# Modulation sums moved wholly beside the first block, their first steps on ScalarE, and the first gated feed-forward's first row group by seven

## Chip, cores and metric

One NeuronCore of a Trainium2 chip runs one program (five engines, 16 DMA engines). The metric is the device time of one execution in microseconds (us).

## What is computed

Two blocks in float32 on x of 512 tokens by 1024 channels. The first block (gMLP and HGRN2 branches, mixed) ends in a feed-forward and a norm:

```
x = x + mix @ w_out
h = rmsnorm(x, norm_ffn)
x = x + square(relu(h @ w_ff1)) @ w_ff2          # 4096 hidden columns
return rmsnorm(x, final_norm)
```

The second has two layers, each a gated feed-forward, a mixer, and a gated feed-forward, all modulated by a vector c:

```
c_act = silu(c)
mod = c_act @ w_ada[l] + b_ada[l]                # 9 x 1024 numbers a layer: shift, scale, gate
h = rmsnorm(x, norm_g[l, 0]) * (1 + sc1) + sh1
x = x + 0.5 * g1 * ((silu(h @ wg) * (h @ wu)) @ wd)   # 2816 hidden columns
```

The modulation of both layers depends on c alone, so it can be computed beside other work.

## The kernel before

**Products.** Every product in float32 is three matmuls: high by high, low by high, high by low, where high is a rounding to fp32r (ScalarE: w_hi, b_hi) and low the rest (VectorE: w_lo, b_lo). The channels lie on the partitions, so a matmul has 512 tokens as its columns. The work is cut into units of 256 output columns by 1024 rows of weights: 1 MB of weights, 48 matmuls of 512 columns. For a unit SP loads w_raw (one of two slots), ScalarE makes w_hi in two halves (`weight_hi`, L1509), VectorE w_lo in two halves (`weight_lo`, L2307), TensorE multiplies into one of two pairs of PSUM banks (`product`, L741). Semaphores count: raw_landed, hi_done, lo_done, chunk_done, out_taken. SP loads unit u+2 when w_lo of unit u is done.

**The first block's feed-forward** is four groups of eight units (`hidden_group`: TensorE L1071, ScalarE L1892, VectorE L2853). In the first four of a group ScalarE takes the output up (Relu), makes w_hi half, squares it into hid and b_hi, makes the other half; VectorE makes w_lo half, b_lo (L2860), w_lo half. The other four units are down products; the first of them takes its rows k in order and waits for b_lo k // 2 before rows k. The last group's four down units are in `residual` (L2387), which adds into xT, and beside it adds up the squares of the next norm (`add_squares`, `add_sixth`). The last of them (`product_tail`, L794) is split so that the norm's sum of squares (L812, L814) runs inside it. The second block's norm "00" is folded with the first block's final norm; plain_ssq is the other sum that this takes, and `final_norm_step` (L2879, eight steps) scales xT afterwards.

**The modulation sums.** For each of 8 quarters q (2304 columns each) there are 8 steps: `ada_acc = ada_in * c_act[:, 0]` (L2770), then seven times `ada_acc += ada_in * c_act[:, k]` (L2773), all on VectorE. Then a turn (L2782, transpose in 32 x 32 blocks) and a reduction (L2789), a small matmul (L1063, `modulation`) and a bias (`add_bias`, L2798). POOL loads ada_in (1.15 MB, two buffers): load o waits for step o-2 (L710). When the steps are made is written out by hand: ADA[u] is the number of steps done by the end of place u, where places 0 to 3 are the output projection's units, 4 to 35 the 32 units of the first block's feed-forward, and from 36 on the first gated feed-forward. `ada_part(u)` (L2820) stands at the end of VectorE's work for a unit. ADA stands at 56 for places 31 to 35, and the last eight steps lie in the first gated feed-forward.

**Gated feed-forwards.** 2816 columns are three groups of 8, 8 and 6 chunks of 128: a group has n/2 pairs (a gate unit, an up unit) and then four down units. A pair can be computed plainly or "by seven" (Strassen's seven block products in Winograd's form, `seven_products` L1151): 14 block products of 12 matmuls with 256 columns instead of 96 with 512. This takes sums of weight blocks and of token blocks t1 to t4 and sums of the results on VectorE. `seven_from(l, j, g)` says from which pair of a group this is done: from the third pair in the first group (two plain pairs let the token sums be made), from the first in the others. The exception is the very first group (0, 0, 0): all four pairs are plain there, the eight last modulation steps and the final norm's steps lie beside them, and the token sums are made from a_hi + a_lo beside its down units (`product_sums`).

The order of instructions on each engine is the order of the program; all waits are explicit, so what stands behind a waiting instruction on its engine waits too.

## Time and profile before

| | us |
|---|---|
| runs, median (lowest to highest) | 2638.23 (2637.9 to 2640.33) |
| the profiled execution, its own time | 2636.77 |
| its span, first to last instruction | 2635.0 |
| TensorE busy | 2615.9 (99%), 15665 matmuls |
| VectorE (DVE) busy | 1836.9 (70%) |
| ScalarE (ACT) busy | 1141.4 (43%) |
| GpSimd (POOL) busy | 71.3 (3%) |

Shares of busy time are means over all stages. The granted TensorE clock is 1.000 of full in the mean. In the text PE is TensorE, PEld its weight loads, DVE VectorE, ACT ScalarE, POOL GpSimd, SP the engine that issues weight loads. "Idle before" in a row is the engine's idle time before the instructions, with what ended it. In a timeline a row is start, duration of the merged instructions, engine, line, operation, out<-in, shapes, count.

### The profile page before, as it was taken

To read this page: it belongs to the slowest core of one execution; us is meant where nothing else is said; L and a number is where in the kernel's file an instruction comes from. 1 tells how busy PE (TensorE), PEld (TensorE's weight loads), DVE (VectorE), ACT (ScalarE), POOL (GpSimd) and SP (SyncE) were. 2 spreads that over 40 slices of the span, in tenths; PEclk is the share of its full clock that TensorE was granted. 3 is DMA by queue.
4 is the path that set the end of the run, shared out by engine and by line. 5 is a ranking of instruction groups with operands and counts; after the bars stand their busy time and mean duration, and the time that the engine had idled before them with its cause. 6 is when DMAs were issued, how large, how long until landed. Compare 5 with 4: busy or idle time off the path is not lost.

```text
span 2635.0 us, 38697 instructions
## 1 busy us (share of the span) xinstructions
PE 2615.9 (99%) x15665; PEld 2302.0 (87%) x15665; DVE 1836.9 (70%) x2347; ACT 1141.4 (43%) x1594; POOL 71.3 (3%) x119
## 2 busy tenths in 40 slices
PE   8999999999999999999999999999999999999999
PEld 7888888888888889998878999989899988898998
DVE  7777653688988779586467685877677654676775
ACT  5566532433224425344455443445343422453432
POOL 1000000000000000000400000000000000000000
PEclk9999999999999999999999999999999999999999
DMA  4111223568887433323212333223233222233332
GB/s 146 65 64 64 83 94 96 185 241 303 306 305 280 162 135 110 96 89 110 64 53 92 112 96 113 89 90 111 95 114 97 96 96 96 87 106 104 105 96 80
DMA packets 257945, 324.56 MB, mean 123 GB/s; under 512 B 5766, under 2 KB 248708, under 8 KB 249604
## 3 DMA queue, kind: packets, MB, share of 16 engines
q1 hardware_dynamic: 245904, 245.12, 28.9%
q0 software_dynamic: 9216, 75.50, 7.6%
q8 instruction: 108, 1.77, 0.3%
q10 hardware_dynamic: 2676, 1.84, 0.2%
q14 instruction: 41, 0.34, 0.0%
HBM read 320.34 MB, written 2.10 MB: 122 GB/s over the span
## 4 chain that ended last, share of the span: by engine, by line
PE 96%; DVE 2%; ACT 1%; issue 0%; DMA 0%; DVEq 0%; ACTq 0%
PE po L764 16%; PE po L766 16%; PE po L765 16%; PE po L1140 7%; PE po L1142 7%; PE po L1141 7%; PE po L833 1%; PE pm L1140 1%; PE pm L1141 1%; PE pm L1142 1%; PE po L835 1%; PE po L848 1%; PE po L881 1%; PE po L867 1%; PE po L876 1%; PE po L934 1%
## 5 line engine op out<-in xcount | busy, mean ns | idle before, releaser
L2312 DVE TENSOR_TENSOR w_lo<-w_raw,w_hi 128x1024 fp32r<-128x1024 f32 x336 | 400.1, 1223 | 146.1 <-ACT w_hi L1517 139.4
L1517 ACT ACTIVATE w_hi<-w_raw 128x1024 fp32r<-128x1024 f32 x290 | 293.0, 1051 | 463.7 <-PE po L766 425.7
L764 PE MATMUL po<-b_hi,w_hi 128*128 128x512 f32 x1008 | 393.0, 390 | 0.0
L765 PE MATMUL po<-b_lo,w_hi 128*128 128x512 f32 x1008 | 392.3, 389 | 0.0
L766 PE MATMUL po<-b_hi,w_lo 128*128 128x512 f32 x1008 | 392.2, 389 | 0.0
L764 PE MATMUL po<-a_hi,w_hi 128*128 128x512 f32 x752 | 293.1, 390 | 0.0
L766 PE MATMUL po<-a_hi,w_lo 128*128 128x512 f32 x752 | 292.6, 389 | 0.0
L765 PE MATMUL po<-a_lo,w_hi 128*128 128x512 f32 x752 | 292.6, 389 | 0.0
L764 PEld LDWEIGHTS po<-b_hi,w_hi 128*128 128x128 f32 x1008 | 189.3, 188 | 39.6 <-DVE b_lo L2860 0.6
L766 PEld LDWEIGHTS po<-b_hi,w_lo 128*128 128x128 f32 x1008 | 189.2, 188 | 39.5
L765 PEld LDWEIGHTS po<-b_lo,w_hi 128*128 128x128 f32 x1008 | 189.3, 188 | 38.6
L2401 DVE SCALAR_TENSOR_TENSOR xT<-po,gate,xT 128x512 f32<-128x512 f32 x104 | 74.0, 734 | 182.1 <-PE po L766 173.1
L766 PEld LDWEIGHTS po<-a_hi,w_lo 128*128 128x128 f32 x752 | 141.2, 188 | 29.3
L765 PEld LDWEIGHTS po<-a_lo,w_hi 128*128 128x128 f32 x752 | 141.2, 188 | 29.2
L764 PEld LDWEIGHTS po<-a_hi,w_hi 128*128 128x128 f32 x752 | 141.2, 188 | 29.2
L1928 ACT ACTIVATE w_hi<-w_raw 128x1024 fp32r<-128x1024 f32 x102 | 106.7, 1056 | 131.9 <-PE po L766 74.0
L2773 DVE SCALAR_TENSOR_TENSOR ada_acc<-ada_in,c_act,ada_acc 128x2304 f32<-128x2304 f32 x56 | 146.4, 2614 | 23.2 <-DMA ada_in<-in_w_ada_dram 21.3
L2929 DVE TENSOR_TENSOR w_lo<-w_raw,w_hi 128x1024 fp32r<-128x1024 f32 x102 | 124.1, 1220 | 36.6 <-ACT w_hi L1928 36.6
L1970 ACT ACTIVATE ev<-po 128x256 f32<-128x256 f32 x204 | 76.8, 377 | 145.0 <-PE po L1142 144.0
L1928 ACT ACTIVATE x_hi<-w_raw 128x1024 fp32r<-128x1024 f32 x102 | 104.2, 1054 | 49.9 <-DVE w_raw L2953 48.8
L2929 DVE TENSOR_TENSOR x_lo<-w_raw,x_hi 128x1024 fp32r<-128x1024 f32 x102 | 122.3, 1218 | 4.7 <-ACT x_hi L1928 4.2
L1140 PE MATMUL po<-t_hi,w_hi 128*128 128x256 f32 x408 | 115.7, 284 | 0.0
(486 smaller groups left out, 6306.8 us busy)
## 6 DMA issues: line engine op xcount, KB each, us to landing
ada_in<-in_w_ada_dram POOLq DMA_DIRECT2D x64, 1152.0 KB, 5.6
w_raw<-in_ffn_wg_dram SPq DMA_DIRECT2D x44, 1024.0 KB, 5.3
w_raw<-in_ffn_wu_dram SPq DMA_DIRECT2D x44, 1024.0 KB, 5.3
w_raw<-in_w_ff_dram SPq DMA_DIRECT2D x32, 1024.0 KB, 5.3
w_raw<-in_ffn_wd_dram SPq DMA_DIRECT2D x32, 1024.0 KB, 5.2
w_raw<-in_w_in_dram SPq DMA_DIRECT2D x27, 1024.0 KB, 5.0
w_raw<-in_ffn_wd_dram SPq DMA_DIRECT2D x16, 768.0 KB, 4.5
w_raw<-in_w_in_c_dram SPq DMA_DIRECT2D x12, 1024.0 KB, 5.1
```

The lines of the kernel that those rows point to most:

```text
L764: pe.matmul(o, wh, hi[:, k, :], start=(k == ks[0]), stop=False)
L765: pe.matmul(o, wh, lo[:, k, :], start=False, stop=False)
L766: mm = pe.matmul(o, wl, hi[:, k, :], start=False, stop=(k == ks[-1]))
L1140: pe.matmul(o, wh[:, c], hi[:, k, :], start=(start and k == 0), stop=False, skip_group_check=True)
L1141: pe.matmul(o, wh[:, c], lo[:, k, :], start=False, stop=False, skip_group_check=True)
L1142: mm = pe.matmul(o, wl[:, c], hi[:, k, :], start=False, stop=(k == 3), skip_group_check=True)
L1517: act.activation(w_hi[:, s, part], w_raw[:, s, part], ACT.Copy).then_inc(hi_done, 1)
L1928: ins = act.activation(batch_out(ring_hi(batch), batch), batch_raw(batch), ACT.Copy)
L1970: act.activation(ev[:, 1, q * QT:(q + 1) * QT], first_bank(s), ACT.Copy)\
L2312: dve.tensor_tensor(w_lo[:, s, part], w_raw[:, s, part], w_hi[:, s, part].bitcast(F32), ALU.subtract).then_inc(lo_done, 1)
L2773: ins = dve.scalar_tensor_tensor(ada_acc[:, :], ada_in[:, k % 2, :], c_act[:, k:k + 1], ada_acc[:, :], ALU.mult, ALU.add)
L2929: ins = dve.tensor_tensor(batch_out(ring_lo(batch), batch), batch_raw(batch), batch_out(ring_hi(batch), batch).bitcast(F32), ALU.subtract)
```

## The change

1. The eight first steps of the modulation sums go from VectorE to ScalarE (`ada_start`): one before the norm "ffn", seven at the end of ScalarE's work for one unit each. POOL's load after next and VectorE's step 1 now wait for them.
2. ADA is new: 2, 4, 5, 5, 6, 9, then two more at each place from 6 (11) to 32 (63), 64 at 33. The last turn is at place 33, the last reduction at 34 (beside the last down units of the first block).
3. The group (0, 0, 0) goes like the other first groups: pairs 3 and 4 by seven, token sums from the norm's rows (`raw_sums`, `sums_hi`, `sums_lo`). `product_sums` and its ScalarE part go. The final norm's steps 0 to 3 stand behind `sums_lo`, 4 to 7 behind the last low block before the first pair by seven.
4. The ScalarE loop over three hidden groups is written out; plain_rstd has a place of its own.

```diff
     def seven_from(l, j, g):
-        if (l, j, g) == (0, 0, 0):
-            return GROUPS[g] // 2
         return PLAIN_PAIRS if g == 0 else 0
...
-    ADA = [1, 2, 3, 3, 4, 5, 7, 9, 10, 13, 15, 17, 18, 21, 23, 25, 26, 29, 31, 33, 34, 37, 39, 40, 41, 43, 45, 48, 49, 51, 53, 56, 56, 56, 56, 56, 57, 58, 60, 62, 64, 64, 64, 64]
+    ADA = [2, 4, 5, 5, 6, 9] + [11 + 2 * n for n in range(27)] + [64, 64, 64]
+    ADA_END = 33
...
                 elif o >= 2:
-                    pool.wait_ge(s_ada, o - 1)
+                    qp, kp = (o - 2) // DK, (o - 2) % DK
+                    if kp == 0:
+                        pool.wait_ge(s_ada_act, ada_first.after("a0", qp))
+                    else:
+                        pool.wait_ge(s_ada, ada.after(f"a{kp}", qp))
...
+            def ada_start(q):
+
+                act.wait_ge(ada_landed[0], q * 8 * DK + 16)
+                if q:
+                    act.wait_ge(s_asum, asum.after("tr", q - 1))
+                act.activation(ada_acc[:, :], ada_in[:, 0, :], ACT.Copy, scale=c_act[:, 0:1])\
+                    .then_inc(s_ada_act, ada_first.one("a0"))
+
+            ada_start(0)
             norm_halves("ffn", U_OUT)
 
+            ADA_START = {ada_unit(DK * q) + 1: q for q in range(1, 2 * FFG)}
...
+                    if ADA_FF + 8 * g + k in ADA_START:
+                        ada_start(ADA_START[ADA_FF + 8 * g + k])
...
             def add_ada(q, k):
 
                 dve.wait_ge(ada_landed[k % 2], at(q, 8 * DK, 16 * (k // 2 + 1)))
-                if k == 0:
...
+                if k == 1:
+                    dve.wait_ge(s_ada_act, ada_first.after("a0", q))
                 else:
                     dve.wait_ge(s_ada, ada.after(f"a{k - 1}", q))
...
-                    add_ada(q, k)
+                    if k:
+                        add_ada(q, k)
+                if u == ADA_END:
+                    turn_ada(2 * FFG - 1)
+                if u == ADA_END + 1:
+                    sum_ada(2 * FFG - 1)
...
                     if last:
                         block_lo(3, l, j, g, i + 1)
+                        if (l, j, g) == (0, 0, 0):
+                            for k in range(DK // 2, DK):
+                                final_norm_step(k)
                         continue
...
                     if i == 0:
                         sums_lo(l, j)
+                        if (l, j, g) == (0, 0, 0):
+                            for k in range(DK // 2):
+                                final_norm_step(k)
```

With this ADA the seven later first steps fall on places 6, 10, 14, 18, 22, 26 and 30: by turns the third hidden unit and the third down unit of each group. Steps 1 and 2 of the same quarter and the reduction of the quarter before fall on the same place on VectorE.

## Rows read from the trace of the kernel before

**Rows 1.** The page's chain that ended last, by engine.

```profile
PE 96%; DVE 2%; ACT 1%; issue 0%; DMA 0%; DVEq 0%; ACTq 0%
```

**Rows 2.** Windows: stretch; length, busy time and count by engine, clock, DMA share.

```profile
583.88:605.64 21.76, 21.76 (x99) 18.01 (x98) 18.38 (x13) 4.02 (x4) 2.64 (x5) 1.00 0.83 296
1429.80:1451.56 21.76, 21.76 (x97) 18.02 (x96) 18.52 (x25) 12.94 (x18) 0.00 (x0) 1.00 0.30 96
1451.56:1491.87 40.31, 40.31 (x337) 40.31 (x336) 30.72 (x42) 21.91 (x34) 0.00 (x0) 1.00 0.40 131
1004.11:1085.03 80.92, 80.92 (x675) 80.78 (x674) 65.90 (x93) 42.75 (x66) 0.00 (x0) 1.00 0.37 118
1535.42:1616.05 80.63, 80.63 (x673) 80.63 (x672) 65.09 (x92) 43.49 (x66) 0.00 (x0) 1.00 0.37 118
```

**Rows 3.** Groups by line on VectorE: count, busy us, mean ns.

```profile
L2773 DVE SCALAR_TENSOR_TENSOR ada_acc<-ada_in,c_act,ada_acc 128x2304 f32<-128x2304 f32 x56 | 146.4, 2614 | 23.2 <-DMA ada_in<-in_w_ada_dram 21.3
...
L2782 DVE STREAM_TRANSPOSE ada_tr<-ada_acc 128x2304 f32<-128x2304 f32 x8 | 20.6, 2575 | 0.1
L2789 DVE TENSOR_REDUCE ada_red<-ada_tr 128x72 f32<-128x2304 f32 x8 | 20.4, 2546 | 0.1
...
L2883 DVE SCALAR_TENSOR_TENSOR xT<-xT,cols,plain 128x512 f32<-128x512 f32 x8 | 5.5, 745 | 0.0
```

**Rows 4.** Timeline of ScalarE, third hidden unit of the last group.

```profile
814.42 1.03 ACT L1897 ACTIVATE ev<-po 128x1024 f32<-128x1024 f32 x1 [6.06 <-PE po L766]
...
817.24 1.05 ACT L1903 ACTIVATE b_hi<-ev 128x1024 fp32r<-128x1024 f32 x1
818.19 1.05 ACT L1517 ACTIVATE w_hi<-w_raw 128x1024 fp32r<-128x1024 f32 x1
```

**Rows 5.** Groups by line and shape on ScalarE.

```profile
L1517 ACT ACTIVATE w_hi<-w_raw 128x1024 fp32r<-128x1024 f32 x290 | 293.0, 1051 | 463.7 <-PE po L766 425.7 <-PE po L848 21.0 <-PE po L881 12.6
...
L1530 ACT ACTIVATE sq<-xT 128x512 f32<-128x512 f32 x49 | 28.5, 620 | 31.1 <-DVE xT L2400 16.9 <-DVE xT L2401 14.2
```

**Rows 6.** Timelines at 486 us; landings of L580 there, of L711 there and at 472; the page's median.

```profile
486.18 1.41 DVE L2770 TENSOR_SCALAR ada_acc<-ada_in,c_act 128x2304 f32<-128x2304 f32 x1
...
486.42 11.26 SPq L580 DMA_DIRECT2D w_raw<-in_w_ff_dram  x2
...
487.89 0.53 POOL L711 DMA_DIRECT2D ada_in<-in_w_ada_dram  x1 [14.45 <-DVE ada_acc L2770]
...
DMA to landing us min/median/max: 5.3/5.3/5.3
...
DMA to landing us min/median/max: 7.6/7.6/7.6
...
DMA to landing us min/median/max: 8.0/9.5/11.1
...
ada_in<-in_w_ada_dram POOLq DMA_DIRECT2D x64, 1152.0 KB, 5.6
```

**Rows 7.** Timelines of VectorE and TensorE at 745 us, a group's first down product.

```profile
744.49 1.22 DVE L2860 TENSOR_TENSOR b_lo<-hid,b_hi 128x1024 fp32r<-128x1024 f32 x1
...
745.76 0.50 PE L764 MATMUL po<-b_hi,w_hi 128*128 128x512 f32 x1
```

**Rows 8.** Windows: the first block's last down units, to the last full addition.

```profile
844.65:864.98 20.33, 20.33 (x96) 16.84 (x95) 18.33 (x25) 7.53 (x10) 0.03 (x1) 1.00 0.59 183
```

**Rows 9.** Timeline of TensorE, the norm's sum of squares.

```profile
867.53 0.69 PE L812 MATMUL pm<-stats,ones 128*128 128x256 f32 x2
```

**Rows 10.** Timeline of VectorE, twin group (0, 1, 0), last plain pair and first by seven.

```profile
1442.06 2.36 DVE L2929 TENSOR_TENSOR w_lo<-w_raw,w_hi 128x1024 fp32r<-128x1024 f32 x2 [2.69 <-ACT w_hi L1928]
...
1455.23 0.41 DVE L3068 TENSOR_TENSOR ev<-ev,pm 128x256 f32<-128x256 f32 x1
...
1456.69 1.22 DVE L3038 TENSOR_TENSOR a_lo<-sq,a_hi 128x1024 fp32r<-128x1024 f32 x1
...
1459.08 0.42 DVE L3068 TENSOR_TENSOR hid<-ev,pm 128x256 f32<-128x256 f32 x1
```

More of the change, by code:

```diff
@@ L260, in hybrid_two_block_kernel @@
         ada_red = ar("ada_red", [P, AQ // 32], F32, 80.5)
[L261 to L262 removed]
+        plain_ssq = ar("plain_ssq", [P, S], F32, 38)[:, :]
+        plain_rstd = ar("plain_rstd", [P, S], F32, 78)[:, :]
         quarter_sums = ar("quarter_sums", [P, P], F32, 80)
@@ L444, in hybrid_two_block_kernel @@
         ff_dve = Steps(s_f_dve, [f"lo{v}" for v in range(4)], reps=FFG, base=1)
-        ada = Steps(s_ada, [f"a{k}" for k in range(DK)], reps=2 * FFG)
+        ada = Steps(s_ada, [f"a{k}" for k in range(1, DK)], reps=2 * FFG)
+        ada_first = Steps(s_ada_act, ["a0"], reps=2 * FFG)
         asum = Steps(s_asum, ["tr", "rd"], reps=2 * FFG)
@@ L1907, in hidden_group @@
                         weight_hi(g * 8 + (U_FF + 2 + k), s=k % 2)
-            with act.Fori(0, FFG - 1) as g:
+                    if ADA_FF + 8 * g + k in ADA_START:
+                        ada_start(ADA_START[ADA_FF + 8 * g + k])
+            for g in range(FFG - 1):
                 hidden_group(g)
@@ L2083, in ffn @@
                 for g, n in enumerate(GROUPS):
[L2084 to L2102 removed]
+                    seven_group(l, j, g, n)
                 return U_FFN[l, j, len(GROUPS) - 1] + GROUPS[-1]
@@ L2961, in raw_sums @@
                 dve.wait_ge(s_n_dve, norm_dve[f"{l}{2 * j}"].after(f"t{DK - 1}b"))
+                if (l, j) == (0, 0):
+                    dve.wait_ge(s_fin_dve, fin_dve.after(f"p{DK - 1}"))
                 def both(step, out_, a, b, op):
@@ L3218, in ffn @@
                 for g, n in enumerate(GROUPS):
-                    fd, fa = ffn_dve[l, j, g], ffn_act[l, j, g]
-                    def pair(i):
-                        un = i * 2 + U_FFN[l, j, g]
-                        weight_lo(un + 2, s=0)
-                        ada_part(ADA_FFN + 2 * i)
-                        for k in range(max(3 * i - 3, 0), min(3 * i, DK)):
-                            final_norm_step(k)
-                        done(un + 1)
-                        dve.wait_ge(out_taken[0], un + 4)
-                        dve.wait_ge(s_w_dve, fd.before(i))
-                        dve.tensor_tensor(hid[:, :], ev[:, 0, :], po[:, 1, :, :].rearrange("p b n -> p (b n)"),
-                                          ALU.mult).then_inc(out_taken[1], 2)
-                        weight_lo(un + 3, (0,), s=1)
-                        dve.wait_ge(s_w_act, fa.after("hi", i))
-                        dve.tensor_tensor(b_lo[:, ds(i * 2, 2), :].rearrange("p b n -> p (b n)"), hid[:, :],
-                                          b_hi[:, ds(i * 2, 2), :].rearrange("p b n -> p (b n)").bitcast(F32),
-                                          ALU.subtract).then_inc(s_w_dve, fd.one("lo"))
-                        weight_lo(un + 3, (1,), s=1)
-                        ada_part(ADA_FFN + 2 * i + 1)
-                    if (l, j, g) == (0, 0, 0):
-                        for i in range(n // 2):
-                            pair(i)
-                        turn_ada(2 * FFG - 1)
-                        sum_ada(2 * FFG - 1)
-                    else:
-                        seven_group(l, j, g, n)
+                    seven_group(l, j, g, n)
                     last = g == len(GROUPS) - 1
```

79 lines of the change are left out of this document (5 added, 74 removed).

## The prediction

> **What bounds the kernel.** I read the page first: the chain that ended last is 96% PE [rows 1], of a span of 2635.0 us. So a change gains what it takes from TensorE's matmuls, and costs what it makes TensorE wait. Then the windows: plain pairs and pairs by seven both run without a hole at the full clock (PEclk 1.00), and beside them VectorE is busy for 18.4 of 21.8 us in the first block's feed-forward and DMA 83% [rows 2]. VectorE is the engine to watch.
>
> **What is gained.** A plain pair of units takes 21.76 us, two pairs by seven 40.31 [rows 2]. Two plain pairs become two by seven: 2 x 21.76 - 40.31 = 3.2 us less. The second row group of the same layer takes 80.92 us where its twin in the next layer takes 80.63 [rows 2]; it now opens like the twin: 0.3 less. The product sums beside the first down projection go too, but VectorE and ScalarE have no matmul waiting for them there: nothing. The number of modulation products on TensorE stays at eight.
>
> **What moves: the sums' work on VectorE.** One step of a sum is 2.61 us, a turn 2.58, a reduction 2.55 [rows 3]; the first step, 1.41 on VectorE [rows 6], goes to ScalarE eight times. Before, all steps but eight fell in the first block, and none beside its last down projection (ADA stands at 56 there). Now the schedule is two steps a unit without a stop; the last three steps, the last turn and the last reduction lie beside that down projection.
>
> **Cost 1, the third hidden unit of each group.** There the sequence is: ScalarE's first step, VectorE's reduction, steps 1 and 2. Let T be the end of that unit's product, 814.3 in the last group. ScalarE takes its output up at 814.42, has the high half of the hidden values at 818.29 and ends its own block at 819.24 [rows 4], T+4.9. VectorE's b_lo and the second low half follow the 818.29, each 1.22 [rows 7]: T+6.4. ScalarE's step over 2304 columns is in no row; 512 columns take 0.620 and 1024 take 1.051 [rows 5], 0.84 ns a column more, so an estimate of 1.05 + 1280 x 0.84 ns = 2.1 us: T+7.0. The load for step 2 waits for it, where before it waited for a VectorE step one unit earlier. POOL issues 0.3 us after a step's end (487.89 after 486.18 + 1.41 [rows 6]): T+7.3. But SP issues the next weight load 0.2 after VectorE is through with the low half (486.42, where VectorE went on to its next work at 486.18 [rows 6]), so a little past T+6.5. How long a sum's load takes then is the unknown. Median 5.6 with nothing close by; 7.6 when it came 1.5 us behind a weight load; 8.0 as the first of two behind a weight load, the second, issued 0.8 later, after 11.1, so in 3.9 behind the first [rows 6]. From below T+12.9, from above T+16 (weight load in at T+11.8, then 3.9); I take 7.7, by the rows nearest to a gap of 0.8: T+15.0. VectorE needs its reduction and step 1 until T+11.5, waits, and ends step 2 at T+17.6. Queued behind it are the next unit's weight low half, and b_lo of the fourth hidden unit. Their two instructions end 2.3 us on: T+19.9. TensorE wants that b_lo after 36 matmuls of 0.227 us in the first down product, which starts at T+10.9: T+19.05. It really does wait there for b_lo: in one group of before it resumed at 745.76, when b_lo (744.49 plus 1.22) was done [rows 7]. So 0.9 us in each of four groups: 3.6, less 0.1 that is there now. Bounds: 0 (load in 5.6) and 4 x 1.9 = 7.6.
>
> A rule on the size: the Trainium skill, "DMA: Bandwidth & Descriptors", section on queues, rings and completion order, says an engine goes round-robin between queue rows packet by packet; then a weight load and a sum's load would slow each other alike. The trace does not quite agree: the weight load issued at 486.42 was in after 5.3 us although the other came behind it, and only the other was late [rows 6]. By the fixed 2.0 us plus bytes at 436 GB/s that the same page of the Trainium skill gives, both loads would be in 7.1 us after the first issue (an estimate), and the stall would vanish.
>
> In the fifth to eighth units the same lateness meets no b_lo, and weights are a unit ahead. The two new steps beside the output projection (before the first norm) find VectorE idle: nothing.
>
> **Cost 2, the last down projection of the first block.** Before, from the block's first addition into xT to the one that releases the last squares, VectorE took 20.33 us, 18.33 of it busy [rows 8]. That last addition ended with the stretch, at 864.98, and the sum's product started at 867.53 without a hole [rows 9]; a square (0.6) and an addition (0.5) lie between and 0.1 for the signals, so there were 1.3 us of slack. Now: the last group's step 2 ends at 814.3 + 17.6 = 831.9; w_lo, b_lo, w_lo 3.5 (1.22 each [rows 7], overlapping by 0.09) and two steps 5.3 bring VectorE to 840.7. On top of 18.33 come two steps 5.3, a bias 0.7, one step and the turn 5.2, the reduction 2.5: 32.0, and no idle time is left. The addition ends at 872.7, ScalarE squares (0.6), VectorE adds (0.5): TensorE can start its sum at 873.9 instead of 867.5: 6.4, of which 0.9 is counted above (TensorE is then that late itself): 5.5 us. The norm's chain hangs on it one to one. From below 4.3 (with the quick load, everything is 2.1 earlier), from above 6.
>
> **Cost 3, the first pair by seven.** Before the pair stand four steps of the first block's final norm, 0.745 us each [rows 3], 2.65 overlapped. The other four go behind the token sums, into a gap of 2.7 us (2.69 in the twin [rows 10]): nothing. In the twin, a pair starts at 1451.56 [rows 2] and each block product is 12 x 0.12 = 1.44 us. The fifth wants the first gate block at 1457.3: it ends at 1455.64 [rows 10], with 2.65 at 1458.3: stall 1.0. The sixth wants a_lo, 1457.91 plus 2.65 = 1460.6, against 1458.8 + 1.0: 0.8. The seventh wants the first up block, 1459.50 plus 2.65 = 1462.2, against 1460.2 + 1.8: 0.2. Sum 2.0 us; bounds 0 and 2.65.
>
> **Sum.** -3.2 - 0.3 + 3.5 + 5.5 + 2.0 = +7.5 us. The profiled execution took 2636.77 us (span 2635.0); that gives 2644.3. The median of the runs lies 1.5 above the profiled one: 2638.23 + 7.5 = 2645.7.
>
> **Rivals.**
> 1. *The sum's load is not held up* (5.6 us, as the median row). Cost 1 vanishes, cost 2 falls to 4.3: -3.5 - 0.1 + 4.3 + 2.0 = +2.7, 2640.9 us, not to be told from no change. For it: 5.6 is the median of 64 [rows 6]. Against: here the two issues are closer together than in either of the late rows. (The Trainium skill's round-robin rule in "DMA: Bandwidth & Descriptors", with its figures, comes out at this rival.)
> 2. *Not slower: the last down projection does not bind.* It decides whether VectorE has added the seventh chunk into xT by 866.2. If it has (the entry to this stretch 6 us earlier than I count, or the reduction skipped past), TensorE runs through, and if the final norm's steps also fit: -3.5 alone, 2634.7. For it: before, VectorE entered at 844.65 and was still in time [rows 8, 9]; mine enters at 840.7. Against: 13.7 us of new work against 4 us of earlier entry, 2 of idle time and 1.3 of slack leaves over 6.
> 3. *Loads stand in line fully* (T+16 and more). Cost 1 grows to 7.6, cost 2 keeps 5.5 to 6, and every step pair waits: about +11 to +12, 2650. For it: 3.9 us from landing to landing at the start. Against: the 7.6 row.
>
> **Chances.** Forecast 0.55, its own range 2642 to 2649; rival 1 0.20; rival 2 0.12; rival 3 0.13. The range reaches from 2637 to 2651, which leaves out rival 2 and half of rival 3. A measurement of this kernel tells 0.2% (5.3 us) from no change. Slower by more: nine in ten of the forecast's 0.55 and rival 3: 0.62; within: rival 1, rival 2 and the rest, 0.36; faster by more 0.02, since all the gain there is makes 0.13%.
>
> **What would show it.** In the changed kernel: two pairs by seven in 40.3 us plus about 2 at their opening; a PE wait for DVE b_lo of about 1 us in the first down product of each of four groups; ScalarE's first step near 2.1 us and the load behind it landing 7 to 8 us after issue; the norm's sum product 5 to 6 us late behind DVE, with no VectorE idle time in that stretch. Wrong if that product starts with VectorE long ready, or if the weights themselves come late.

## The result, and the profile after

The changed kernel takes 2647.2 us, median of 8 runs (2645.57 to 2648.69); the kernel before, on the same chip, 2638.09 (8 runs, 2637.61 to 2640.33). The ratio is 1.0034, 95% interval [1.0025, 1.0043]: slower by 9.1 us, and by more than the 0.2% that I had set as the bound. The profiled execution has a span of 2645.5 us against 2635.0, 10.5 more.

The page's chain that ended last, of the changed kernel:

```profile
PE 90%; DVE 5%; DMA 2%; ACT 2%; issue 1%; DVEq 0%; SPq 0%; ACTq 0%
```

Before it was PE for 96% [rows 1]. Now VectorE and DMA stand in it: the path leaves TensorE. These shares say where the path runs, not what it costs; where TensorE stands still, the view of waits tells (TensorE's, 525 to 1245 us; columns are waiting tile and line, what ended the wait, us in total, times, longest):

```profile
PE pm L815 <- DVE stats L2334: 5.9, 1, 5.9
PE po L767 <- DVE b_lo L2846: 1.4, 3, 0.6
PE po L1143 <- issue: 0.9, 1, 0.9
PE po L836 <- ACT a_hi L1548: 0.7, 1, 0.7
PE po L1143 <- DVE a_lo L2989: 0.7, 1, 0.7
PE po L1143 <- ACT ev L1983: 0.6, 1, 0.6
PE po L1143 <- DVE ev L3025: 0.3, 1, 0.3
```

In the kernel before the same view of the same stretch has one row, the 0.7 us on a_hi (under another line number). So there are three new places: the norm's sum product at the end of the first block (L815), b_lo in the first down products (L767), and the opening of the first pair by seven (the 0.9 on "issue", a wait whose releaser the profile doesn't show, and the 0.7 on a_lo). The last two rows are in the second row group and turn out to be chance (below).

**Third hidden unit of a group.** Timelines of POOL, SP, ScalarE and VectorE around 735 us (columns: start, duration, engine, line, operation, tiles, shapes, count, idle before):

```profile
727.77 1.03 ACT L1908 ACTIVATE ev<-po 128x1024 f32<-128x1024 f32 x1 [6.06 <-PE po L769]
...
732.49 2.21 ACT L1895 ACTIVATE ada_acc<-ada_in,c_act 128x2304 f32<-128x2304 f32 x1
...
734.20 0.37 SPq L579 DMA_DIRECT2D w_raw<-in_w_ff_dram  x1
...
734.99 0.53 POOL L714 DMA_DIRECT2D ada_in<-in_w_ada_dram  x1 [8.48 <-ACT ada_acc L1895]
...
736.41 2.60 DVE L2755 SCALAR_TENSOR_TENSOR ada_acc<-ada_in,c_act,ada_acc 128x2304 f32<-128x2304 f32 x1
742.54 2.62 DVE L2755 SCALAR_TENSOR_TENSOR ada_acc<-ada_in,c_act,ada_acc 128x2304 f32<-128x2304 f32 x1 [3.52 <-DMA ada_in<-in_w_ada_dram]
745.07 1.22 DVE L2296 TENSOR_TENSOR w_lo<-w_raw,w_hi 128x1024 fp32r<-128x1024 f32 x1
746.21 1.22 DVE L2846 TENSOR_TENSOR b_lo<-hid,b_hi 128x1024 fp32r<-128x1024 f32 x1
```

With T = 727.65 (ScalarE takes the unit's output up 0.12 after its end, as in [rows 4]): ScalarE's first step ends at T+7.05 (predicted T+7.0), POOL issues at T+7.3 (predicted 7.3), 0.8 behind SP. VectorE waits 3.5 us for that load, and b_lo of the fourth unit is done at T+19.8 (predicted 19.9). The load itself, in the view of that one DMA, and the weight load ahead of it:

```profile
DMA to landing us min/median/max: 7.5/7.5/7.5
...
DMA to landing us min/median/max: 5.0/5.0/5.0
```

7.5 us where I took 7.7; the weight load issued just ahead of it took 5.0, undisturbed.

**The last down projection of the block.** Timelines of VectorE and of TensorE:

```profile
842.28 1.29 DVE L2384 TENSOR_TENSOR xT<-po,xT 128x512 f32<-128x512 f32 x2
...
846.20 2.62 DVE L2755 SCALAR_TENSOR_TENSOR ada_acc<-ada_in,c_act,ada_acc 128x2304 f32<-128x2304 f32 x1 [0.36 <-DMA ada_in<-in_w_ada_dram]
849.04 2.62 DVE L2755 SCALAR_TENSOR_TENSOR ada_acc<-ada_in,c_act,ada_acc 128x2304 f32<-128x2304 f32 x1 [0.22 <-DMA ada_in<-in_w_ada_dram]
...
866.77 2.35 DVE L2296 TENSOR_TENSOR w_lo<-w_raw,w_hi 128x1024 fp32r<-128x1024 f32 x2
869.03 2.54 DVE L2770 TENSOR_REDUCE ada_red<-ada_tr 128x72 f32<-128x2304 f32 x1
871.50 0.74 DVE L2308 SCALAR_TENSOR_TENSOR stats<-sq,square_gain,stats 128x512 f32<-128x512 f32 x1
...
874.02 1.01 DVE L2384 TENSOR_TENSOR xT<-po,xT 128x512 f32<-128x512 f32 x2
875.47 0.88 DVE L2334 SCALAR_TENSOR_TENSOR stats<-sq,square_gain,stats 128x256 f32<-128x256 f32 x2 [0.43 <-ACT sq L1531]
```

```profile
869.85 0.28 PE L812 MATMUL pm<-b_hi,w_lo 128*128 128x256 f32 x1
876.01 1.22 PE L815 MATMUL pm<-stats,ones 128*128 128x256 f32 x2 [5.88 <-DVE stats L2334]
```

From the first addition into xT (842.28) to the last full one (874.02) VectorE stands still only for two sum loads, 0.36 and 0.22 us; then it waits 0.43 for ScalarE's square. TensorE stands still for 5.9 us; before, this product (then L812) began without a hole at 867.53 [rows 9].

**What stands behind it.** Windows of the same stretch (length, busy time and count by engine, granted clock, DMA share, GB/s):

```profile
868.00:872.00 4.00, 2.12 (x18) 1.92 (x16) 4.00 (x3) 0.00 (x0) 0.00 (x0) 1.00 0.32 86
872.00:876.00 4.00, 0.00 (x0) 0.00 (x0) 3.56 (x8) 0.94 (x2) 0.00 (x0) 0.74 0.51 176
876.00:880.00 4.00, 3.99 (x14) 3.63 (x15) 1.80 (x4) 1.23 (x3) 0.00 (x0) 0.50 0.00 0
880.00:884.00 4.00, 3.89 (x28) 3.60 (x26) 2.83 (x8) 2.91 (x8) 0.00 (x0) 0.90 0.00 0
```

The granted clock, 1.00 everywhere in [rows 2], is 0.50 in the window in which TensorE begins again: 14 matmuls in four busy microseconds, half rate, the 1.2 GHz level. From the norm's sum product (876.01) to the product over the plain squares (894.91, L873) it is 18.90 us; before it was 16.94 (867.53 to 884.47). That is 2.0 us which no term of my sum has. The Trainium skill, "TensorE: Matmul & The Clock Gate", Part 1, says that the gate lets half of the pulses through after idleness and that activity releases it; the trace agrees: 1.00 at 868 to 872, 0.74 in the wait, 0.50 behind it, 0.90 at 880 to 884. My forecast had the stall and no price for what follows it.

The whole difference, profile to profile, in four stretches cut at products that both kernels have (starts from TensorE's timelines; the wait is counted here from start to start, which gives 6.0 where the view has 5.9):

| stretch | before | after | difference |
|---|---|---|---|
| start to the feed-forward norm's sum | 516.8 | 517.0 | +0.2 |
| from there to TensorE's arrival at the next norm's sum | 350.8 | 353.0 | +2.2 |
| wait at that product | 0 | 6.0 | +6.0 |
| from it to the product over the plain squares | 16.9 | 18.9 | +2.0 |
| from there to the next norm's sum product | 336.5 | 336.5 | +0.1 |

Behind that nothing changes. The last row is made of four parts, which the experiments take apart.

### The profile page after: what moved, and what is told of

Its sections match the earlier page's. It is cut to its first block, busy times and chain, and to the rows that moved or that the text cites. A ratio compares the mean times of both kernels' runs of the same rounds, so it can differ in the third digit from the quotient of the medians.

```text
span 2645.5 us, 39021 instructions
## 1 busy us (share of the span) xinstructions
PE 2616.3 (99%) x15809; PEld 2308.1 (87%) x15809; DVE 1844.9 (70%) x2383; ACT 1166.9 (44%) x1627; POOL 71.2 (3%) x119
## 4 chain that ended last, share of the span: by engine, by line
PE 90%; DVE 5%; DMA 2%; ACT 2%; issue 1%; DVEq 0%; SPq 0%; ACTq 0%
PE po L767 14%; PE po L769 14%; PE po L768 14%; PE po L1143 8%; PE po L1145 8%; PE po L1144 8%; DMA ada_in<-in_w_ada_dram 1%; PE po L836 1%; PE pm L1144 1%; PE pm L1143 1%; PE pm L1145 1%; PE po L838 1%; PE po L851 1%; PE po L884 1%; PE po L879 1%
## 5 line engine op out<-in xcount | busy, mean ns | idle before, releaser
L1518 ACT ACTIVATE w_hi<-w_raw 128x1024 fp32r<-128x1024 f32 x278 | 280.7, 1051 | 436.1 <-PE po L769 398.0
L767 PE MATMUL po<-b_hi,w_hi 128*128 128x512 f32 x1008 | 393.3, 390 | 1.5 <-DVE b_lo L2846 1.4
L767 PE MATMUL po<-a_hi,w_hi 128*128 128x512 f32 x688 | 268.1, 390 | 0.0
L769 PE MATMUL po<-a_hi,w_lo 128*128 128x512 f32 x688 | 267.7, 389 | 0.0
L768 PE MATMUL po<-a_lo,w_hi 128*128 128x512 f32 x688 | 267.7, 389 | 0.0
L767 PEld LDWEIGHTS po<-b_hi,w_hi 128*128 128x128 f32 x1008 | 189.2, 188 | 42.0 <-DVE b_lo L2846 3.2
L1941 ACT ACTIVATE w_hi<-w_raw 128x1024 fp32r<-128x1024 f32 x108 | 112.9, 1056 | 148.1 <-PE po L769 85.0
L769 PEld LDWEIGHTS po<-a_hi,w_lo 128*128 128x128 f32 x688 | 129.1, 188 | 27.0
L768 PEld LDWEIGHTS po<-a_lo,w_hi 128*128 128x128 f32 x688 | 129.2, 188 | 26.7
L767 PEld LDWEIGHTS po<-a_hi,w_hi 128*128 128x128 f32 x688 | 129.1, 188 | 26.5
L1941 ACT ACTIVATE x_hi<-w_raw 128x1024 fp32r<-128x1024 f32 x108 | 110.3, 1054 | 54.0 <-DVE w_raw L2939 52.9
L2915 DVE TENSOR_TENSOR x_lo<-w_raw,x_hi 128x1024 fp32r<-128x1024 f32 x108 | 129.6, 1218 | 4.7 <-ACT x_hi L1941 4.2
L1143 PE MATMUL po<-t_hi,w_hi 128*128 128x256 f32 x432 | 122.5, 284 | 1.0 <-issue 0.9
```

The source lines that it names most:

```text
L767: pe.matmul(o, wh, hi[:, k, :], start=(k == ks[0]), stop=False)
L768: pe.matmul(o, wh, lo[:, k, :], start=False, stop=False)
L769: mm = pe.matmul(o, wl, hi[:, k, :], start=False, stop=(k == ks[-1]))
L1143: pe.matmul(o, wh[:, c], hi[:, k, :], start=(start and k == 0), stop=False, skip_group_check=True)
L1518: act.activation(w_hi[:, s, part], w_raw[:, s, part], ACT.Copy).then_inc(hi_done, 1)
L1941: ins = act.activation(batch_out(ring_hi(batch), batch), batch_raw(batch), ACT.Copy)
```

## The experiments

All are edits of the changed kernel; what is given is the median, the ratio to the kernel before in the same set, and the profiled span. My theory going in: three causes of lateness (the load of step 2 held back by ScalarE's first step; five long VectorE instructions beside the last down projection; four norm steps ahead of the first pair by seven) and, as a fourth cost, the fall of the clock behind the second. The three rivals: DMA is simply full, VectorE's lateness enters from the groups ahead, the opening is bound by something else.

### e1: the five instructions beside the last down projection, made small

```
-                        add_ada(q, k)
+                        add_ada(q, k, 32 if u >= 32 else AQ)
...
-                    turn_ada(2 * FFG - 1)
+                    turn_ada(2 * FFG - 1, 32)
...
-                    sum_ada(2 * FFG - 1)
+                    sum_ada(2 * FFG - 1, 32)
```

(the last argument is the number of columns)

> The changed kernel, but beside the last down projection of the first block (places 32 to 34 of the schedule) the last three steps, the last turn and the last reduction of the sums treat 32 columns instead of 2304; every wait, every load and every signal stays. Left out by this is part of the eighth modulation sum. My theory: these five instructions (2.6 us each) are what makes VectorE late for the norm's last addition, and the 5.9 us that TensorE then waits is also what lets its clock fall to the lower level behind, another 2.0 us. So the wait is 0 to 0.3 us, TensorE's sum product starts near 869.9 in the trace and the first product of the gated feed-forward 11.9 us behind it instead of 13.9: 7.9 us less than the changed kernel (2645.5 us of span becomes 2637.6). Rival A, the clock has another cause: 5.9 less, product to first product still 13.9. Rival B, the lateness comes in with the block (VectorE enters the stretch late by the lost waits of the groups ahead) and not from these five: 0 to 2 us less.

Measured: median 2638.29 us, ratio 0.9999 [0.9989, 1.0008], span 2635.9. TensorE's timeline at the sum product and at the product over the plain squares:

```profile
870.05 0.48 PE L815 MATMUL pm<-stats,ones 128*128 128x256 f32 x1
...
887.01 0.59 PE L873 MATMUL pm<-plain_ssq,ones 128*128 128x512 f32 x1
```

The wait is gone and the 16.96 us behind it are back. The last steps, turn and reduction of the eighth sum treat 32 of 2304 columns here, so this kernel leaves out most of that work. It entered the stretch as late as the changed kernel (b_lo waits 2.7 us), so rival B is out: without the five instructions the late entry alone makes no wait. The span is 9.6 less, 7.9 as expected and 1.7 from the last stretch of the table, where TensorE now needs 334.8 instead of 336.5 us although nothing was edited there. That 1.7 is followed up in e12.

### e2: the second four norm steps moved into the last pair by seven

```
@@ seven_group, after the last plain pair
-                        if (l, j, g) == (0, 0, 0):
-                            for k in range(DK // 2, DK):
-                                final_norm_step(k)
@@ seven_taken, after first_block("u", ...)
+                if (l, j, g) == (0, 0, 0) and not more:
+                    for k in range(DK // 2, DK):
+                        final_norm_step(k)
```

> The changed kernel, but the second four steps of the first block's final norm leave their place ahead of the first pair by seven and go into the last pair by seven of the same row group, which has no blocks of a next pair to prepare. My theory: the two waits of TensorE at the opening of the first pair (1.07 and 0.82 us in the trace) are due to those four steps; both go (under 0.2 left) and nothing comes in the last pair, where VectorE has room for 2.65 us: 1.9 us less than the changed kernel. Rival A, the opening is bound by the token sums or by ScalarE: the waits stay, 0 less. Rival B, the last pair has no room: the waits go, and a wait for the hidden values of that pair comes of up to 2.65: 0 to 1 more.

Measured: median 2644.57 us, ratio 1.0025 [1.0015, 1.0034], span 2642.8. TensorE's waits, same view and stretch as above:

```profile
PE pm L815 <- DVE stats L2334: 6.1, 1, 6.1
PE po L767 <- DVE b_lo L2846: 2.2, 3, 1.0
PE po L836 <- ACT a_hi L1548: 0.7, 1, 0.7
```

Both waits at the opening are gone, nothing new has come. From the product over the plain squares to the next norm's sum it takes 332.7 us (895.65 to 1228.38), against 334.8 in e1, e3, e5, e8 and e12, which have the norm steps in their place: 2.1 us for the term that I had at 2.0. VectorE really has room in the last pair:

```profile
954.66 2.73 DVE L2869 SCALAR_TENSOR_TENSOR xT<-xT,cols,plain_rstd 128x512 f32<-128x512 f32 x4
960.12 0.42 DVE L3025 TENSOR_TENSOR ev<-ev,po 128x256 f32<-128x256 f32 x1 [2.73 <-ACT ev L1983]
```

### e3: a third buffer for the sums' inputs

```
+        ada_in3 = ar("ada_in3", [P, AQ], F32, 39)
...
-                elif o >= 2:
-                    qp, kp = (o - 2) // DK, (o - 2) % DK
+                elif o >= 3:
+                    qp, kp = (o - 3) // DK, (o - 3) % DK
```

(and a third semaphore; a step's buffer is its number modulo 3; the plain squares' sum moves 2 KB down)

> The changed kernel with a third 9 KB buffer for the sums' inputs, so that the load for step o waits for step o-3 instead of o-2; nothing else moves. My theory: TensorE's waits for b_lo in the first down product of each group (0.54, 0.25, 0.65 and 0.72 us) come from the load of step 2, which is held back until ScalarE has read the first step and so lands late. With a third buffer it is issued earlier, all four waits go (2.2 us), and VectorE no longer waits in front of its steps, so it enters the last down projection about 4 us earlier and the 5.9 us wait there falls to about 2 (the work of that stretch is the same), with the clock held at its upper level behind it if the wait is short enough: 6 to 8 us less than the changed kernel. Rival A, DMA is the limit and not the buffer (a pair of 1.1 MB loads and the weights fill the unit of 10.9 us): waits for b_lo stay, within 1 us of the changed kernel. Rival B, only the b_lo waits go and the end stays bound by work: 2.2 us less.

Measured: median 2639.33 us, ratio 1.0004 [0.9995, 1.0013], span 2638.4, 7.0 less than the changed kernel's first profile (of which 1.7 is chance, see e12), 7.9 less by the medians. The terms that the two profiles show make 5.6 of it: 2.2 of b_lo waits, 2.6 of the wait at the sum product, 0.8 of the clock. TensorE's waits:

```profile
PE pm L820 <- DVE stats L2339: 3.3, 1, 3.3
PE po L1148 <- issue: 0.9, 1, 0.9
...
PE po L1148 <- DVE a_lo L2994: 0.7, 1, 0.7
```

No wait for b_lo is left, so rival A falls: DMA had room for all of it. Rival B (the b_lo waits alone, 2.2 us) falls too. In the same unit POOL's load now stands a step ahead, and VectorE runs on without the hole of 3.5 us:

```profile
735.31 5.33 DVE L2760 SCALAR_TENSOR_TENSOR ada_acc<-ada_in,c_act,ada_acc 128x2304 f32<-128x2304 f32 x2
740.56 1.22 DVE L2301 TENSOR_TENSOR w_lo<-w_raw,w_hi 128x1024 fp32r<-128x1024 f32 x1
741.69 1.22 DVE L2851 TENSOR_TENSOR b_lo<-hid,b_hi 128x1024 fp32r<-128x1024 f32 x1
```

The loads themselves got slower, median 7.0 us to landing against 5.7 in the changed kernel, and it doesn't matter: each has a step more of time. The last wait falls to 3.3 where I expected 2, and even that lets the clock fall (0.77 and 0.80 in the windows 868 to 872 and 872 to 876): sum product to plain squares 18.1 us (870.59 to 888.71), 1.2 over. So the earlier entry is worth 2.6 of 5.9 us there. The rest is the work beside that projection: e6 and e7 take it away piece by piece.

### e4: the first steps back on VectorE, two buffers

```
                 if k == 0:
+                    dve.tensor_scalar(ada_acc[:, :], ada_in[:, 0, :], c_act[:, 0:1], None, ALU.mult)\
+                        .then_inc(s_ada, ada.one("a0"))
```

(`ada_start` and its calls on ScalarE taken out)

> The changed kernel with the first steps of all eight sums back on VectorE (1.4 us each, as in the kernel before), two buffers, schedule and all else as changed. It parts two readings of the waits for b_lo in the third hidden unit: that ScalarE's late first step holds the load back, or that two steps a unit are too many for two buffers whoever does the first. My theory is the first: the four waits (2.2 us in the changed kernel's trace, 3.4 in two later ones) vanish, VectorE enters the last down projection earlier although it has 11 us more to do in all, and the wait at the sum product falls from 5.9 to 3.5 (worked out from instruction times), with some 1.2 us of lower clock behind it as the run with three buffers had for 3.3: in all 4.5 to 6 us less than the changed kernel, span 2640. Rival A (two steps a unit are too many for two buffers): the waits for b_lo stay, and VectorE's 1.4 us more per sum come on top: 0 to 4 us more than the changed kernel.

Measured: median 2642.3 us, ratio 1.0016 [1.0007, 1.0025], span 2642.0. TensorE's waits:

```profile
PE pm L811 <- DVE stats L2318: 3.7, 1, 3.7
PE pm L1062 <- DVE ada_red L2757: 1.6, 1, 1.6
...
```

The b_lo waits vanish with ScalarE's step, as they do with the third buffer. Two edits that have nothing in common but the moment at which the load of step 2 may go both remove them; two steps a unit are not too many for two buffers. New is one wait of 1.6 us of a modulation product for its reduction, which I had not foreseen, and the fall of the clock behind 3.7 us of waiting was dearer than I put it (872.77 to 891.89: 19.1, 2.2 over). So the span of the profiled execution came out 2 above the 2640 expected; it is one of the slower ones, and the median span of the 11 runs is 2640.5.

### e5 and e8: TensorE kept busy through the wait

The same addition at two places of `product_tail`, for this norm only:

```
+                    for m in range(24):
+                        pe.matmul(pm[:, 3, :], w_hi[:, slot, 0:P], hi[:, m % kc, :], start=True, stop=True)
```

> The changed kernel, with 24 more matmuls of 512 columns on TensorE (0.227 us each, 5.4 us; their result is read by nobody) at the end of the last down projection of the first block, where TensorE waits 5.9 us for VectorE's last addition. My theory: the wait is filled, TensorE's sum product starts when it did (876.0 in the trace), and the granted clock stays at 1.00 behind it instead of falling to 0.50 for some 6 us; the first product of the feed-forward comes 11.9 us behind the sum product and not 13.9: 2.0 us less than the changed kernel. Rival, the 2.0 us are not the clock's but another engine's (VectorE or ScalarE work that sits behind the lateness): the clock stays up and the time stays the same within 0.3 us. If the filling itself delays the sum product: up to 0.3 more.

Measured: median 2654.44 us, ratio 1.0057 [1.0043, 1.0071], span 2652.6. A miss of mine: TensorE waits behind the third step of the last half chunk (L814), and I put the matmuls ahead of the wait at the end of the unit, where there was nothing left to wait for. The wait stayed (6.8 us), the clock fell, and the product over the plain squares came 24.8 us behind the sum product, 5.9 more than in the changed kernel; the 24 matmuls are 5.4 of it. It shows only that TensorE's own work in that stretch is on the path in full. e8 puts them at the right place.

> The 24 extra matmuls again (5.4 us, read by nobody), now at the place where TensorE really waits: ahead of the norm's sum product, which stands behind the third step of the last half chunk and not at the end of the down projection. In the run before they stood behind it and TensorE did 5.9 us more, with the wait kept. My theory: TensorE's wait (5.9 us in the changed kernel) shrinks to about 0.5, the sum product starts when VectorE has added, as before (876 to 877 in the trace), the granted clock stays at 1.00 behind it, and from the sum product to the product over the plain squares it is 16.9 us as in the kernel before, not 18.9: 2.0 us less than the changed kernel (about 2643.5 of span). Rival: the 2.0 us belong to VectorE's and ScalarE's late work, not to the clock: 18.9 stays and the time is that of the changed kernel.

Measured: median 2645.99 us, ratio 1.003 [1.0019, 1.0041], span 2643.7. TensorE's timeline, then windows:

```profile
875.79 1.29 PE L817 MATMUL pm<-b_hi,w_hi 128*128 128x512 f32 x5
877.82 0.70 PE L819 MATMUL pm<-stats,ones 128*128 128x256 f32 x2 [0.73 <-DVE stats L2338]
```

```profile
872.00:876.00 4.00, 4.00 (x19) 3.31 (x18) 4.00 (x6) 0.00 (x0) 0.00 (x0) 1.00 0.82 262
876.00:880.00 4.00, 3.27 (x20) 2.64 (x19) 2.33 (x5) 1.83 (x4) 0.00 (x0) 1.00 0.00 0
```

The sum product starts as late as in e5 (877.8 and 877.9), whose b_lo waits are like this one's; VectorE's and ScalarE's late work ahead of it is the same, and yet the product over the plain squares (L877, at 894.79) comes 16.97 us behind it, not 18.90. The clock is at 1.00 throughout. So the 2.0 us are the clock's, and only the clock's. The span, 1.8 less than that of the changed kernel's first profile, is no measure of it: 1.9 less is the clock's and 1.7 the chance that e12 shows, and against them the sum product starts 1.8 later, mostly from b_lo waits of 3.4 us instead of 2.2.

### e12: the changed kernel once more

> The changed kernel itself once more, unaltered, for what in its profile is chance. Its first profile shows two things that no other run of mine has: 1.2 us of waits in the second pair by seven of the second row group (at 1027.6 and 1029.8), where a weight load took 7.9 us instead of 5.3 while an instruction fetch moved through the same DMA engines; and b_lo waits of 2.2 us in all, where the four later runs with the same code in that stretch have 2.7 to 3.5. My theory: both are chance, the median stays at 2646 to 2647; in this profile the 1.2 us are gone (the stretch from the product over the plain squares to the sum product of the next norm is 334.8 us instead of 336.5) and the b_lo waits come to 2.7 to 3.5. Rival: the 1.2 us come from the layout of this very program, return in the same place, and are a part of the 9 us that I had not counted.

Measured: median 2647.68 us, ratio 1.0038 [1.0024, 1.0051], span 2647.4. The waits in the second row group are not there, and the last stretch takes 334.8 us (898.38 to 1233.21), so 1.7 us of the first profile were chance. They are not tied to this kernel either: e13, below, has 0.3 and 0.3 us of them, and e4 comes 0.5 us late in the same row group. What started them in the first profile was a weight load issued at 1019.07, which took 7.9 us; the view of that one DMA (who waited for it: us, times; then its landing):

```profile
  ACT w_hi L1941: 3.0, 1
...
DMA to landing us min/median/max: 7.9/7.9/7.9
```

Two packets of instruction fetch lay beside it, but the same two lie beside this load in e12, where it took 5.8 us; in e13 it took 7.5. So the fetch alone doesn't make it late, and the cause stays open. The b_lo waits come to 2.3 us in this profile, a little below the 2.7 to 3.5 I expected: they vary from run to run. This profile's span is long for another reason, at the start: the feed-forward norm's sum is at 520.2 instead of 517.0, 3.2 us later.

### e13: two buffers, with the reduction and all norm steps moved

```
                 if u == ADA_END:
                     turn_ada(2 * FFG - 1)
-                if u == ADA_END + 1:
-                    sum_ada(2 * FFG - 1)
@@ seven_group, first plain pair, after sums_lo
-                            for k in range(DK // 2):
-                                final_norm_step(k)
+                            sum_ada(2 * FFG - 1)
@@ seven_taken, last pair, after first_block("u", ...)
+                    for k in range(DK):
+                        final_norm_step(k)
```

(and ScalarE waits for the reduction before it writes over its source)

> The changed kernel with its two buffers and its own schedule, but with the eighth reduction moved out of the last down projection (to behind the token sums) and all eight final norm steps in the last pair by seven. Expected against the run that moved only four norm steps (2642.8 of span): b_lo waits as there (about 3 us), the wait at the sum product 6.2 less 2.5 = 3.6, the clock still falls behind it (1.2 to 2.1, as in the runs with waits of 3.3 and 3.8), nothing at the pairs: 2.5 to 3.3 less, span 2639.5 to 2640.3. So without the third buffer the change stays slower than the kernel before by 4 to 5 us. Rival: VectorE's lateness is not additive there (something else, a load, sets the last addition), and less than 1.5 us comes back.

Measured: median 2642.16 us, ratio 1.0015 [1.0006, 1.0024], span 2640.7. The wait at the sum product is 3.8 us (6.1 in e2, 2.5 us of work taken out), the clock falls behind it (874.24 to 892.47: 18.2), and there is nothing at the opening of the pairs. The last stretch is 334.1 us, 1.3 over e2, with 0.6 of waits in the second row group as in the changed kernel's first profile. VectorE's lateness there adds up instruction by instruction.

### e6: third buffer, four norm steps late, a denser schedule

```
-    ADA = [2, 4, 5, 5, 6, 9] + [11 + 2 * n for n in range(27)] + [64, 64, 64]
+    ADA = [2, 4, 5, 5] + [7 + 2 * n for n in range(14)] + [37, 39, 41, 43, 45, 46, 48, 50, 52, 55, 57, 58, 60, 62, 64] + [64] * 3
```

(with the edits of e2 and e3)

> Both repairs together and a denser schedule: third buffer for the sums' inputs, the second half of the final norm's steps in the last pair by seven, and the last steps of the sums taken one place earlier (schedule 2, 4, 5, 5, then 7 to 33 by twos, 37 to 45 by twos, 46, 48, 50, 52, 55, 57, 58, 60, 62, 64), so that beside the last down projection stand two steps, the turn and the reduction instead of three, the turn and the reduction. Expected: no waits for b_lo (as with three buffers), the wait at the sum product down from 3.3 to about 1.9 us, with less of the clock's fall behind it (under 1.2), no waits at the opening of the pairs by seven (1.9 less): from the 2638.4 of the three-buffer run 3.7 to 4.5 less, span 2634 to 2634.7, median about 0.5 to 1 under the kernel before. Rival: the places with three and four steps make VectorE late for b_lo or for a modulation product, and it comes out at 2636 to 2638.

Measured: median 2634.02 us, ratio 0.9986 [0.9977, 0.9995], span 2631.8: better than expected by 2 us. The only wait left in the block, in the view of TensorE's waits from 800 to 880 us:

```profile
PE pm L820 <- DVE stats L2339: 1.1, 1, 1.1
```

1.1 us instead of 1.9, and behind it the clock stays at 1.00: sum product to plain squares 16.96 us (868.05 to 885.01). A short stall costs itself and no more. These two are what I had sized too high.

### e7: the same with the reduction out of the way

> As the run before it in this list, and the eighth sum's reduction (2.5 us on VectorE) moves from beside the last down projection to behind the token sums in the first plain pair of the gated feed-forward; the four final norm steps that stood there join the other four in the last pair by seven, where VectorE has 2.7 us idle in one piece and 3.5 more in pieces. Expected: the wait at the sum product (about 1.9 us in that kernel) vanishes, the clock stays at 1.00, nothing new in the pairs: 2 to 3 us less than that kernel, span about 2632, 2.5 to 3.5 us (0.1%) less than the kernel before. Rival: eight norm steps (5.3 us) in the last pair delay its up or gate block, and 0 to 1.5 us of it come back as a wait of TensorE there or in the down projection behind it.

Measured: median 2632.65 us (11 runs, 2632.38 to 2633.14), ratio 0.998 [0.9971, 0.9989], span 2630.6. From 525 us to the next norm TensorE waits for nothing but the 0.7 us on a_hi that every kernel has:

```profile
PE po L841 <- ACT a_hi L1553: 0.7, 1, 0.7
```

It is 5.3 us faster than the kernel before by the medians (2637.98 in this set) and 4.4 by the spans. 3.7 of that is the last stretch, the change's own gain with its costs taken away; the third buffer and the denser schedule are part of this kernel too. Against e6 it is 1.2 us in span, the wait, and not 2 to 3. Eight norm steps in the last pair delay nothing: the last stretch stays at 332.7 us (883.80 to 1216.53).

### e14: e7 with the first steps on VectorE

> The fastest kernel so far (third buffer, denser schedule, late reduction, late norm steps; span 2630.6) with the first steps of all eight sums on VectorE again instead of ScalarE: 1.4 us each, 11 us more for VectorE in the block. My theory: ScalarE's share of the steps was only needed because of the two buffers' chain, or not at all; with the third buffer VectorE has the room, and the time is the same within 0.5 us. Rival A: VectorE is too full (it is busy for nearly the whole of that stretch), so it enters the last down projection late and 1 to 4 us come back there. Rival B: the reduction behind VectorE's own first step comes later, and the modulation product or b_lo of the third unit waits for it, as the one modulation product in the run with two buffers did (1.8 us).

Measured: median 2634.41 us, ratio 0.9987 [0.9978, 0.9996], span 2632.1, 1.5 more than e7. TensorE's waits:

```profile
PE pm L1067 <- DVE ada_red L2764: 0.8, 1, 0.8
```

Rival B, then: a modulation product is late behind VectorE's own first step; and TensorE comes a further 0.2 us later to the norm's sum. The remaining 0.4 us of the span lie behind the next norm, where nothing was edited. My "same within 0.5 us" was wrong. Once the third buffer is there, ScalarE's share is worth 1.0 us by the places named and 1.8 by the medians of two sets, whose ratios to the kernel before overlap in their intervals; with two buffers it is what made the load late.

The runs side by side (b_lo: distances between the starts of neighbouring matmuls, less the usual 0.227 us, four places together; the next columns are in us too):

| kernel | median | span | b_lo waits | wait at the sum | sum to plain squares | plain squares to next sum |
|---|---|---|---|---|---|---|
| before | 2638.1 | 2635.0 | 0.1 | 0 | 16.9 | 336.5 |
| changed | 2647.2 | 2645.5 | 2.2 | 5.9 | 18.9 | 336.5 |
| e12, changed again | 2647.7 | 2647.4 | 2.3 | 6.5 | 18.4 | 334.8 |
| e1 | 2638.3 | 2635.9 | 2.7 | 0 | 17.0 | 334.8 |
| e2 | 2644.6 | 2642.8 | 3.0 | 6.1 | 18.9 | 332.7 |
| e13 | 2642.2 | 2640.7 | 2.8 | 3.8 | 18.2 | 334.1 |
| e5 | 2654.4 | 2652.6 | 3.5 | 6.8 | 24.8 | 334.8 |
| e8 | 2646.0 | 2643.7 | 3.4 | 0.7 | 17.0 | 334.8 |
| e4 | 2642.3 | 2642.0 | 0 | 3.7 | 19.1 | 335.3 |
| e3 | 2639.3 | 2638.4 | 0 | 3.3 | 18.1 | 334.8 |
| e6 | 2634.0 | 2631.8 | 0 | 1.1 | 17.0 | 332.7 |
| e7 | 2632.7 | 2630.6 | 0 | 0 | 17.0 | 332.7 |
| e14 | 2634.4 | 2632.1 | 0 | 0 | 17.0 | 332.7 |

## Why the prediction was right, and where not

The forecast was +7.5 us, 2645.7; it came to +9.1, 2647.2, inside its own range (2642 to 2649) and on the side given 0.62. Step by step:

- **The gain.** I had -3.2 - 0.3 = -3.5. With the opening clean (e2, e6, e7) the last stretch is 332.7 us against 336.5: -3.7. Right.
- **Cost 3, the norm steps at the opening.** +2.0 forecast; 334.8 against 332.7 is +2.1. Right, and by the mechanism named: e2 moves the four steps and both waits go.
- **Cost 1, b_lo in the third hidden unit.** +3.5 forecast; 2.2 to 3.5 in seven profiles, mean 2.9. In the group read above every link was within 0.2 us of its time (first step, issue, landing after 7.5, b_lo), and e3 and e4 break the chain at two links with the same outcome. The size is a little high, since I let VectorE end and TensorE arrive at the same phase in all four groups; they differ (a group's wait is 0.2 to 1.15 us).
- **Cost 2, the last down projection.** +5.5 forecast, with 4.3 to 6 as bounds; 5.9 to 6.8 in four profiles, mean 6.3. The mechanism is shown by e1 and e13; the size was low by 0.4 to 1.3. TensorE's sum started at 876.0 where I had 873.9. 1.6 of these 2.1 us are VectorE's entry (842.3, not 840.7): I had taken T of the last group from the kernel before, without the lateness of the three groups ahead. TensorE's arrival is late by the same amount (870.0, not 868.4), so the two errors cancel in the stall; what is left in this profile is some 0.4 us. I had written "no idle time is left"; VectorE waits 0.36 and 0.22 us for two sum loads there.
- **What the sum lacked.** I costed the stall at its own length. The clock falls in it (in e13 just behind it) and comes back only some microseconds after TensorE has begun again: +2.0 (1.5 in e12), shown by e8, where filling the wait gives it back. This is the one term missing, and as large as the whole 1.6 us between forecast and result.

With the measured terms (means over the profiles) the sum is -3.7 + 2.9 + 6.3 + 1.8 + 2.1 = 9.4, beside 9.1 and 10.0 measured in the two sets. That the forecast came so near has some luck in it: the errors of its terms (gain 0.2 too small, cost 1 0.6 too high, cost 2 0.8 too low, cost 3 0.1 too low) nearly cancel and leave it 0.1 short, and the missing 1.8 made that 1.9, still inside the range. Profile to profile the difference is 10.5 us, 8.8 without the 1.7 of chance.

**Rival 1** (load not held up) is out: its 5.6 us were 7.5, and in the seven profiles with two buffers and ScalarE's first step the 28 loads of this place took 7.1 to 8.0. Reading the round-robin rule of the Trainium skill ("DMA: Bandwidth & Descriptors", the section on queues, rings and completion order) as the two loads slowing each other alike would have put them in together by 7.1 us after the first issue, an estimate with the fixed 2.0 us and the 436 GB/s that the same page of the Trainium skill gives (section "Anatomy of one DMA"). The first took 5.0 and the second was in 8.3 after it. **Rival 2** (the down projection doesn't bind) is out by 5.9 us.

**Rival 3** (loads fully in line) is out in its size: cost 1 is 2.9 us and not 7.6, the time 2647 and not 2650. Its picture is nearer to the traces than rival 1's. In line would have been 3.9 behind the weights' 739.2, at 743.1; VectorE began the step at 742.54, and over the 28 loads the sum's load landed 2.8 to 3.8 us behind the weights. The load isn't wholly in line, though. In the view of DMA queues from 737.00 to 739.24, just ahead of the weights' landing, both queues move (packets, MB, share of the 16 engines):

```profile
q1 hardware_dynamic: 563, 0.56, 72.2%
q0 software_dynamic: 34, 0.31, 39.1%
```

The first is the weights, the second the sum's load, of which the larger part came behind.

## What to carry to other kernels

Moving work off the engine that looks full can still make it late, if the engine that takes the work over stands late in a chain that frees a buffer: ask when each buffer is freed under the new order, not only how busy each engine is; here a third buffer was worth 8 us by the medians. Put a stall on the matmul engine down with what the clock does behind it: a wait of 1.1 us cost 1.1, waits of 3.3 to 6.5 cost 1.2 to 2.2 more, and not in the order of their length. And side work with no deadline (a norm of the residual, a last reduction) belongs where the profile shows the vector engine idle in one piece, which is the last pair of a group and not its opening.

## What was not expected of the hardware

- The fall of the clock does not grow with the wait: behind 3.3, 3.7, 3.8, 5.9, 6.1 and 6.5 us of idle TensorE the same work took 1.2, 2.2, 1.3, 2.0, 2.0 and 1.5 us more; behind 1.1 us, nothing. It goes with how long the lower level lasts once TensorE has begun again, which the granted clock of the 8 us behind the sum product's start tells (windows from that start; cost is the stretch to the plain squares less 16.96 us, in e5 also less 24 x 0.227):

  | kernel | wait | clock in the 8 us behind it | cost |
  |---|---|---|---|
  | e5 | 6.8 | 0.65 | 2.4 |
  | e4 | 3.7 | 0.67 | 2.2 |
  | e2 | 6.1 | 0.70 | 2.0 |
  | changed | 5.9 | 0.70 | 1.9 |
  | e12 | 6.5 | 0.77 | 1.5 |
  | e13 | 3.8 | 0.79 | 1.3 |
  | e3 | 3.3 | 0.81 | 1.2 |

  Half rate for a part of 8 us takes away 8 x (1 - clock): 2.8 to 1.5 us from e5 to e3, 0.4 to 0.5 more than was measured in each. In e13 the clock is still 1.00 in the first microsecond behind the wait (874.24 to 875.24) and 0.52 in the two after that. What sets the moment of the fall, these runs don't show.
- More loads in flight are each slower (median 5.7 to 7.0 us with a third buffer) and the kernel is 8 us faster for it (2639.3 against 2647.2).
- The two profiles of the same kernel differ by 1.7 us in one stretch that nothing touched, by 0.6 in the wait at the norm's sum, and by 3.2 us at the start. The median of the runs moved by 0.5. A term under 2 us is to be taken from several profiles. Why one weight load in the second row group is sometimes late (7.9 us for 5.3) stays open.
